# Softmax weights and x transposed as pairs of 64-row strips, each strip into its own PSUM bank

## What is computed

```python
def mixer_layer(x, c, k_buf, v_buf, s0, pos0, lb, ...):
    h = rms_norm(x, norm_g) * (1 + scale) + shift        # x: (1, 2048, 1024)
    proj = h @ w_in                                      # contracts over the 1024 columns of h
    ...
    ya = window_attention(qa, k_all, v_all, pos0, sinks) * jax.nn.silu(za)
    ...

def window_attention(q, k_all, v_all, pos0, sinks):      # blocks of 128 queries, 256 keys each
    s = jnp.einsum('bnikgd,bnjkd->bnkgij', qb, kb).astype(jnp.float32) * (d ** -0.5)
    ...                                                  # mask, sink, row maximum
    p = jnp.exp(s - m)
    p = p / (jnp.sum(p, axis=-1, keepdims=True) + jnp.exp(sink - m))
    o = jnp.einsum('bnkgij,bnjkd->bnikgd', p.astype(v_all.dtype), vb)
```

## Time and profile before

| | |
|---|---|
| median of 3 runs | 1715.11 us (1713.58 to 1715.34) |
| the profiled execution, its own time | 1714.18 us |
| its span, first to last instruction | 1712.4 us |
| TensorE matmuls busy | 1638.8 us, 96% |
| TensorE weight loads busy | 1349.6 us, 79% |
| VectorE, ScalarE, GpSimd busy | 46%, 35%, 41% |
| mean granted TensorE clock, of full speed | 0.983 |

### The profile page before, as it was taken

How to read it: one execution, slowest core, us unless ns; L and a number is a source line. 1 busy time by engine, 2 the same in 40 slices (tenths; PEclk the granted TensorE clock), 3 DMA queues, 4 the chain that set the end, 5 groups by cost and what they waited for, 6 DMA issues and landing times.

```text
span 1712.4 us, 31325 instructions
## 1 busy us (share of the span) xinstructions
PE 1638.8 (96%) x13225; PEld 1349.6 (79%) x13225; DVE 789.2 (46%) x1833; ACT 592.9 (35%) x1156; POOL 704.8 (41%) x328
## 2 busy tenths in 40 slices
PE   6979999999899899999999999999999999999998
PEld 2767778877898667887779966888879976788888
DVE  3754444233467664523245855533235755443122
ACT  3325413433322452243332355134341355133330
POOL 1514412354653442335454344225574344134561
PEclk9889999999999999999999999999999999999999
DMA  9703212243753221233244332123445332122342
GB/s 320 202 25 88 74 30 71 88 123 87 214 137 74 81 87 30 81 89 112 85 160 117 84 87 74 40 75 99 123 154 131 97 90 71 45 70 75 111 142 89
DMA packets 299269, 172.62 MB, mean 101 GB/s; under 512 B 73582, under 2 KB 289991, under 8 KB 298088
## 3 DMA queue, kind: packets, MB, share of 16 engines
q1 hardware_dynamic: 299128, 170.61, 34.3%
HBM read 159.66 MB, written 11.96 MB: 100 GB/s over the span
## 4 chain that ended last, share of the span: by engine, by line
PE 84%; DVE 8%; issue 2%; ACT 2%; POOL 1%; DMA 1%; SPq 0%; DVEq 0%
PE ps_D L689 45%; PE ps_D L686 23%; PE ps_XD L742 2%; PE ps_XB L843 2%; PE ps_XB L849 1%; PE ps_XB L815 1%; DMA th_t<-in_w_ada 1%; ACT p_or_hf L1031 1%; PE ps_XA L837 1%; DVE p_or_hf L1353 1%; DVE p_or_hf L1366 1%; DVE ff L1212 1%; PE ps_XA L815 1%; PE ps_XA L867 1%; PE ps_XB L862 1%
## 5 line engine op out<-in xcount | busy, mean ns | idle before, releaser
L1520 POOL TENSOR_TENSOR w_lo_t<-w_raw,w_hi_t 128x1024 fp32r<-128x1024 f32 x232 | 561.7, 2431 | 817.3 <-ACT w_hi_t L893 817.2
L689 PE MATMUL ps_D<-h_hi_t,w_hi_t 128*128 128x512 f32 x1024 | 416.5, 407 | 1.0 <-POOL w_lo_t L1520 1.0
L689 PE MATMUL ps_D<-h_lo_t,w_hi_t 128*128 128x512 f32 x1024 | 401.8, 392 | 0.0
L689 PE MATMUL ps_D<-h_hi_t,w_lo_t 128*128 128x512 f32 x1024 | 400.7, 391 | 0.0
L893 ACT ACTIVATE w_hi_t<-w_raw 128x1024 fp32r<-128x1024 f32 x232 | 240.0, 1050 | 48.9 <-PE ps_D L686 29.4
L689 PEld LDWEIGHTS ps_D<-h_hi_t,w_hi_t 128*128 128x128 f32 x1024 | 193.0, 188 | 60.5 <-issue 23.2
L689 PEld LDWEIGHTS ps_D<-h_hi_t,w_lo_t 128*128 128x128 f32 x1024 | 192.8, 188 | 42.5
L689 PEld LDWEIGHTS ps_D<-h_lo_t,w_hi_t 128*128 128x128 f32 x1024 | 193.3, 189 | 35.9
L686 PE MATMUL ps_D<-w_hi_t,h_hi_t 128*128 128x384 f32 (+1 forms) x384 | 142.9, 372 | 1.6 <-POOL h_lo_t L1525 1.6
L686 PE MATMUL ps_D<-w_hi_t,y_hi_t 128*128 128x384 f32 (+1 forms) x384 | 126.0, 328 | 14.1 <-issue 14.1
L686 PE MATMUL ps_D<-w_hi_t,h_lo_t 128*128 128x384 f32 (+1 forms) x384 | 137.2, 357 | 0.0
(11 more groups left out here) (356 smaller groups left out, 2521.7 us busy)
## 6 DMA issues: line engine op xcount, KB each, us to landing
w_raw<-in_w_in SPq DMA_DIRECT2D x72, 512.0 KB, 3.9
w_raw<-in_w_merge SPq DMA_DIRECT2D x64, 512.0 KB, 4.0
w_raw<-in_w_in SPq DMA_DIRECT2D x64, 256.0 KB, 4.1
w_raw<-in_w_out SPq DMA_DIRECT2D x32, 512.0 KB, 4.6
x_or_AT<-in_x_prompt SPq DMA_DIRECT2D x20, 512.0 KB, 5.3
w_raw<-in_w_proj_a SPq DMA_DIRECT2D x64, 128.0 KB, 3.0
w_raw<-in_w_proj_b SPq DMA_DIRECT2D x32, 256.0 KB, 3.2
xr<-in_x_prompt SPq DMA_DIRECT2D x16, 512.0 KB, 6.6
```

Of the source, the lines that this page charges most:

```text
L689: ins = mm(bank[:, :], w[:, s0, k0 + k, :], a[:, k, :], start=go, stop=end)
L1520: s.done(g_.tensor_tensor(w_lo[:, c], w_raw[:, n % NRAW], f32(w_hi[:, c]), ALU.subtract), "w_lo")
```

## The change

The order of tasks on every engine stays as it is. In `x_turn` and in the task `PT` each transpose of 128x128 becomes two: the first turns rows 0 to 63 of the block, the second rows 64 to 127. Each has a weight load of 64 rows x 128 columns and a moving operand of 64 columns (the 64x64 corner of the identity that belongs to its rows), and writes 128 partitions x 64 columns. The first strips go to the first bank of XA or XB (columns 0 to 511), the second ones to the second bank. So a group has 16 transposes in place of 8, alternating between the upper and the lower half of the array's rows. Reading a block back means to read 64 columns from each bank. The ScalarE copy of XB does that with its access pattern, still as one instruction of 1024 columns, and writes runs of 64 columns. The eight VectorE instructions of `modulate` read two runs of 64 columns each. What lies in SBUF afterwards is the same as before.

```diff
@@ x_turn
                 for k in range(KT):
-                    ins = tr(bank[:, P * k:P * k + P], src[:, P * k:P * k + P], ident[:, :])
+                    for i in range(2):
+                        r, c = slice(64 * i, 64 * i + 64), 512 * i + 64 * k
+                        ins = tr(bank[:, c:c + 64], src[r, P * k:P * k + P], ident[r, r])
                 s.done(ins, f"{BANK[key]}_full")
@@ PE, task PT
                     for kt in range(2):
                         for m in range(M4):
-                            ins = tr(bank[:, 512 * kt + P * m:512 * kt + P * m + P], p_t[:, m, P * kt:P * kt + P],
-                                     ident[:, :])
+                            for i in range(2):
+                                r, c = slice(64 * i, 64 * i + 64), 512 * i + 256 * kt + 64 * m
+                                ins = tr(bank[:, c:c + 64], p_t[r, m, P * kt:P * kt + P], ident[r, r])
@@ ACT, task PT
-                    s.free(fn(PT[:, :, :], XB[:, :].rearrange("p (a b) -> p a b", a=2), ACT.Copy), *key)
+                    s.free(fn(R3[:, :].rearrange("p (k i q) -> p i k q", k=8, i=2),
+                              XB[:, :].rearrange("p (i k q) -> p i k q", i=2, k=8), ACT.Copy), *key)
@@ DVE, modulate
                 for k in range(KT):
-                    ins = ts(hf[t % 2][:, k, :], bank[:, P * k:P * k + P], gscale[:, k, 8:9], shift[:, k, 8:9],
-                             ALU.mult, ALU.add)
+                    ins = ts(hf[t % 2][:, k, :].rearrange("p (i q) -> p i q", i=2),
+                             bank[:, :].rearrange("p (i k q) -> p i k q", i=2, k=KT)[:, :, k, :],
+                             gscale[:, k, 8:9], shift[:, k, 8:9], ALU.mult, ALU.add)
```

## The result

| | before | after |
|---|---|---|
| median | 1716.59 us (13 runs, 1712.91 to 1721.65) | 1720.31 us (13 runs, 1715.88 to 1724.63) |
| ratio after/before, 95% interval | | 1.0025 (1.0014 to 1.0037) |
| profiled execution, its span | 1714.18, 1712.4 us | 1721.87, 1720.1 us |
| mean granted TensorE clock in it | 0.983 | 0.973 |

The forecast was 1704.2 us in a range of 1699 to 1713. The time is above the range, and the sign is wrong.

What follows compares the result with a forecast made beforehand. TensorE's own issue was taken to set the end, matmuls in flight for 96% of the span. Savings of 9.76 + 0.6 + 0.5 = 10.9 us took 1715.1 to 1704.2 us, range 1699 to 1713.

Steps and rivals of the forecast that it cites:

- The step of a pair: In a group of strips: upper and lower rows overlap, so a pair steps at 0.061 us; one whole transpose stepped at 0.109.
- First to last: In a group of 16 strips: 0.48 us from the start of the first strip to that of the last.
- on to the next tiling: After a group's last strip: 0.15 us to the next task of another tiling.
- entry behind dense: From the last dense matmul's start to a group's first strip: 0.32 us, as changing the tiling costs 0.09.
- Rivals 1, 2 and 3: 1: strips take turns, 1725.7 us, chance 0.08; 2: 64-row loads lose transposes' speed, 1722.5 us, 0.06; 3: partial overlap, 1712-1718, 0.11.
- Behind a wait, at the lower clock: Three groups of wait, `PT`, `S` at 1.2 GHz: 1.87 us becomes 1.16 each, 2.13 us saved in all.
- Copy, modulate and weights at no cost: XB copy stays about 1023 ns, `modulate` keeps eight instructions, weight waits add 0 to 1 us.
- x, 0.6 us and 0.5 in the preparation: Groups of `x_turn`: 12 in the iterations save 0.6 us, those in the preparation 0.5 us.
- At unit 60: Three x groups at the start of the 4.4 us wait gain nothing; the last `yf`, not x, ends that wait.
- The sum of 10.9 us: Total saving over all groups on TensorE: 9.76 us, plus 0.6 for x and 0.5 in the preparation.
- rival 4: Gain partly given back at waits for `p_norm` that don't start earlier, or for weights: 4 to 7 us left, chance 0.10.
- Where they fall can move the time by 2 us either way: Some ten lower-clock stretches of a few us after TensorE's waits: their placement shifts the time by 2 us.

Runs made afterwards that it cites:

- experiment 3: VectorE takes the maximum of `S(5)` before `ff` and `kk`: ratio 0.9904 in the changed kernel, 0.9958 in the kernel before, both against the kernel before.
- e9_before_dve_late: Kernel before, with VectorE held up by two one-column memsets ahead of the `ff` of head f3, no strips: 1722.95 us, ratio 1.0027.
- e2_x_only: Strips in `x_turn` and `modulate` only, `PT` and its copy as in the kernel before: 1719.99 us, ratio 1.0009 to the kernel before.
- e8_strips_in_turn: Full change, but each group turns all upper strips before all lower ones: 1723.17 us, ratio 1.0042 to the kernel before.
- e3_after_s_first: Full change, plus VectorE takes the maximum of `S(5)` ahead of `ff` and `kk` of its unit: 1702.31 us, ratio 0.9904 to the kernel before.

## Why the prediction was wrong

- **The step of a pair, 0.061 us: right** (0.062). First to last 0.49 against 0.48, on to the next tiling 0.15 against 0.15, entry behind dense 0.32 against 0.32. Rivals 1, 2 and 3 are out.
- **Behind a wait, at the lower clock**: I had 1.16 us from the first strip to `S`, and it is 578.05 - 577.01 = 1.04 in the rows below. The gain there is a little larger than forecast.

```profile
577.01 1.11 PE L847 MATMUL ps_XB<-ident,p_or_hf 64*128 64x64 f32 x16 [6.16 <-DVE p_or_hf L1371]
578.05 1.32 PE L839 MATMUL ps_XA<-kT,qT_or_szb 64*32 64x160 f32 x32
```

- **Copy, modulate and weights at no cost: right.** The copy of XB takes 1024 ns (1023 in the earlier trace rows), `modulate` 404, the wait for `w_lo` is 3.2 us.
- **x, 0.6 us and 0.5 in the preparation: too small to be seen.** `L653` (`L651` before) starts 0.29 us earlier, at 36.30, for a forecast of 0.4. At unit 60 the gain turned into wait, as the text had it (4.66 against 4.40 us). But the wait is ended by weights that stand behind the `h_lo` of an x tile in GpSimd's queue, and not by the last `yf`.
- **The sum of 10.9 us: right as TensorE's own work,** as far as can be told: 9 us (5 to 13) in experiment 3, where little takes it back.
- **The step that failed is the sentence against rival 4**, "the chain to `p_norm` begins with `S`, which itself moves up". It begins with `S` only where the reader of `S` is idle. Behind `S(5)` stood `ff` and `kk` in VectorE's queue, and the rows of before had a maximum 3.66 us behind its `S`, a `kk` of 2.63 us next to a `ff` of 0.55, and two `w_lo` of 2.5 us beside them. I read none of these rows. They would have pointed to a race in which a shift of 0.3 us between the two engines can cost 2 us or more, three times. Rival 4 named the right waits, but its mechanism, a release of `p_norm` that doesn't come earlier, can take back no more than the strips gain. Here the release came later: the waits grew by 7.8 us. It stood there at 4 to 7 us left and a chance of 0.10. That and the clock took back the whole gain and more.
- **"Where they fall can move the time by 2 us either way": mis-sized.** The clock cost some 7 us, by the estimate above. What I hadn't asked is whether the lower clock is more frequent in the changed kernel on average.

**What stays open.** Why the clock is lower isn't settled. The longer waits account for little of it: `e9_before_dve_late` has them and 0.9805. `e2_x_only` and `e8_strips_in_turn` have the waits for `p_norm` of before and 0.9772 and 0.9755. Nor do the strips do it wherever they stand: under the new order it is 0.9808 with them all (`e3_after_s_first`), 0.9812 with those of `PT` alone and 0.9825 with none, in 4, 6 and 6 executions, a difference within their scatter. With the old order all four kernels with strips are lower by 0.003 to 0.006. What decides how long TensorE stays at half clock behind a wait was not found. In `e8_strips_in_turn` the stretch behind the same `PT(5)`, after a wait of 2.15 us, was at half clock in part:

```profile
1042.00:1046.00 4.00, 2.11 (x10) 1.00 0.62 183
1046.00:1050.00 4.00, 3.74 (x52) 0.70 0.08 23
```

Before, after a wait of 2.28 us, it was at full clock throughout, and in iteration 3, after one of 2.29, at half in part (`PT(5)` took 1.80 us there, where it took 1.06).

## To carry to other kernels

- A gain on the engine that sets the end is only sure between waits. For every wait on the path, read the queue of the engine that ends it from the release backwards, and ask of each instruction whether it takes what it takes alone. One that is 0.55 us at one place and 2.6 at another is a race, and a shift of tenths of a microsecond may lose it, by a speedup as well as by a delay.
- If a sound change costs time, look for the race before dropping it: here one line that puts the awaited work ahead of the contended work turned +0.25% into -0.96%, of which that line alone is worth 0.42% in the old kernel.
- Compare the granted clock over all executions, not of the profiled one alone; here it was a term nearly as large as the edit.

## What the runs showed of the hardware

- Float32 transposes of 64 rows x 128 columns with 64 moving columns start every 0.062 us on the same rows of the array. Upper and lower rows work side by side into two banks, a pair every 0.062. In `e8_strips_in_turn` the first lower strip starts beside the fifth upper one, with three upper ones ahead of it in program order still to come. The records don't name the rows; this is read from the starts, where one comes 0.006 us behind another and two rows of starts 0.062 us apart run on from there.
- Which of VectorE and GpSimd gets the shared port isn't told by the starts of the records alone. `ff` won when it started 0.33 and 0.39 us ahead of `w_lo` (before, `e8_strips_in_turn`), and lost at 0.10 and at 0.02 us ahead (`e9_before_dve_late`, after). The other two iterations of each of these runs say the same: 0.31 to 0.39 us ahead wins, 0.02 to 0.10 loses.
- The custom instruction of the maximum, which reads PSUM, ran in 0.54 us beside a `w_lo`, while `ff` and `kk`, from SBUF to SBUF, were held up.
